# Two attentions with weights turned one step later, and the output product's first tiles begun between the last jobs

## What is computed

```
p = softmax(q @ k.T * scale + bias)          # 256 x 256 per head, causal
o = concat over heads of (p @ v)             # 256 x 1024
h = h + o @ w_out
```

## Time and profile before

| what | us |
|---|---|
| median of 3 runs (lowest, highest) | 1268.11 (1267.1, 1269.16) |
| the profiled execution's own time | 1271.67 |
| span of the profiled execution, first to last instruction | 1269.8 |
| PE busy | 1202.0 (95%) |
| DVE busy | 834.7 (66%) |
| ACT busy | 652.7 (51%) |
| POOL busy | 236.0 (19%) |
| first attention, first scores to last output ready | 90.2 to 147.6 |
| second attention | 424.6 to 458.3 |

### The profile page before, as it was taken

How to read it: one execution, slowest core, us unless ns; L and a number is a source line. 1 busy time by engine, 2 the same in 40 slices (tenths; PEclk the granted TensorE clock), 3 DMA queues, 4 the chain that set the end, 5 groups by cost and what they waited for, 6 DMA issues and landing times.

```text
span 1269.8 us, 19077 instructions
## 1 busy us (share of the span) xinstructions
PE 1202.0 (95%) x7698; PEld 1046.5 (82%) x7698; DVE 834.7 (66%) x1291; ACT 652.7 (51%) x1060; POOL 236.0 (19%) x300
## 2 busy tenths in 40 slices
PE   6898899999999889999999999999998789999996
PEld 5785588888888668888888889999996479888996
DVE  6955586666586567666557876457866856776643
ACT  6436566644333656664446555346545545655531
POOL 4103331110000232111112212000005510111101
PEclk9999999999999999999999999999999789999998
DMA  7790155564453424545554554652441023455461
GB/s 277 263 213 34 39 194 177 188 219 179 168 191 137 167 95 175 194 173 197 199 199 138 194 199 147 206 212 103 167 173 50 1 108 134 174 190 192 147 203 56
DMA packets 34088, 205.56 MB, mean 162 GB/s; under 512 B 3776, under 2 KB 6352, under 8 KB 13776
## 3 DMA queue, kind: packets, MB, share of 16 engines
q1 hardware_dynamic: 30704, 200.47, 44.3%
q10 hardware_dynamic: 3296, 3.87, 1.6%
HBM read 202.87 MB, written 1.46 MB: 161 GB/s over the span
## 4 chain that ended last, share of the span: by engine, by line
PE 79%; DVE 14%; ACT 3%; POOL 2%; issue 1%; DMA 1%; POOLq 0%; ACTq 0%; DVEq 0%
PE ps L662 36%; PE ps L667 23%; PE ps L665 5%; PE ps L666 5%; DVE wl L604 3%; PE ps L686 1%; PE ps L687 1%; PE ps L688 1%; DVE tf L2181 1%; POOL pb L965 1%; PE ps L909 1%; DVE y L1932 1%; DVE xb L740 1%; PE ps L1420 1%; ACT wh L575 1%
## 5 line engine op out<-in xcount | busy, mean ns | idle before, releaser
L604 DVE TENSOR_TENSOR wl<-raw,wh 128x2048 fp32r<-128x2048 f32 (+4 forms) x196 | 421.2, 2154 | 149.7 <-ACT wh L575 149.6
L662 PE MATMUL ps<-xb,wh 128*128 128x512 f32 x1424 | 502.8, 398 | 4.2 <-DVE wl L604 3.7
L667 PE MATMUL ps<-xb,wl 128*128 128x256 f32 x1696 | 477.1, 281 | 0.0
L575 ACT ACTIVATE wh<-raw 128x2048 fp32r<-128x2048 f32 (+4 forms) x196 | 348.5, 1781 | 153.3 <-PE ps L667 119.2
L662 PEld LDWEIGHTS ps<-xb,wh 128*128 128x128 f32 x1424 | 267.3, 188 | 70.5 <-issue 5.4
L667 PEld LDWEIGHTS ps<-xb,wl 128*128 128x128 f32 x1696 | 321.9, 190 | 0.0
L667 PE MATMUL ps<-ab,wl 128*128 128x256 f32 x1088 | 307.4, 283 | 0.0
L662 PE MATMUL ps<-ab,wh 128*128 128x512 f32 x640 | 226.8, 400 | 0.8 <-DVE ab L975 0.8
L667 PEld LDWEIGHTS ps<-ab,wl 128*128 128x128 f32 x1088 | 207.3, 191 | 0.0
L662 PEld LDWEIGHTS ps<-ab,wh 128*128 128x128 f32 x640 | 120.3, 188 | 31.7 <-DVE ab L975 1.4
L859 DVE TENSOR_TENSOR tf<-ps,tf 128x256 f32<-128x256 f32 x148 | 61.9, 421 | 119.6 <-ACT tf L854 119.6
(11 more groups left out here) (322 smaller groups left out, 1332.1 us busy)
## 6 DMA issues: line engine op xcount, KB each, us to landing
raw<-wstream SPq DMA_DIRECT2D x156, 1024.0 KB, 4.8
raw<-wstream SPq DMA_DIRECT2D x32, 704.0 KB, 4.0
raw<-wstream SPq DMA_DIRECT2D x8, 768.0 KB, 4.1
e_bt<-scratch ACTq DMA_DIRECT2D x16, 128.0 KB, 8.6
o_bt<-scratch SPq DMA_DIRECT2D x2, 1024.0 KB, 9.9
raw<-wstream SPq DMA_DIRECT2D x2, 560.0 KB, 7.2
raw<-wstream SPq DMA_DIRECT2D x4, 256.0 KB, 6.7
h<-xt ACTq DMA_DIRECT2D x4, 256.0 KB, 7.8
```

Source lines behind the costliest of these rows:

```text
L575: e.g.activation(WH[i % HLN][:, 0:w], RAW[i % RAWN][:, 0:w], ACT.Copy).then_inc(S["hi"], 1)
L604: e.g.tensor_tensor(WL[q][:, 0:w], RAW[i % RAWN][:, 0:w], f32(WH[q][:, 0:w]), ALU.subtract).then_inc(S["lo"], 1)
L662: e.g.matmul(PS[b][:, :].rearrange("p (a t) -> p a t", a=2), wh[:, sl], x2[:, :, cs], start=start, stop=k == p.nk - 1, skip_group_check=pair)
L667: ins = e.g.matmul(o, wl[:, sl], xh[:, cs], start=False, stop=k == p.nk - 1, skip_group_check=pair)
```

## The change

Turns, copies and outputs of both attentions happen one step later on every engine, the pv groups move from even to odd steps, and the compressed branch's extra work from step 11 to 12. `eo` and `oo` get banks 3 and 4 for their first two tiles, free with the maxima of job 21 (13); the new function `pe_begun` runs 12 of their blocks (k = 0 to 5 of tiles 0 and 1) in three portions of four at steps 22, 24 and 26 (14, 16 and 18), and the product itself starts at its 13th block. Since fixed banks don't advance the ring, all units behind eo take ring places two earlier, all behind oo four earlier.

```diff
-        Gemm("eo", "cols", 8, 8, 16, "h_eo", wide=True),
+        Gemm("eo", "cols", 8, 8, 16, "h_eo", fixed=(3, 4), wide=True),
...
-        Gemm("oo", "cols", 8, 8, 16, "h_oo", wide=True),
+        Gemm("oo", "cols", 8, 8, 16, "h_oo", fixed=(3, 4), wide=True),
...
-            "even": {3: (S["ex"], 24), 4: (S["ex"], 24), 0: (S["ol"], 7), 1: (S["ol"], 8), ...
-            "odd": {3: (S["ex"], 40), 4: (S["ex"], 40), ...
+            "even": {3: (S["mx"], 22), 4: (S["mx"], 22), 0: (S["ol"], 7), 1: (S["ol"], 8), ...
+            "odd": {3: (S["mx"], 38), 4: (S["mx"], 38), ...
-        def pe_cols(e, p, ks, xb, ready, after=None):
+        def pe_cols(e, p, ks, xb, ready, after=None, part=slice(None)):
...
-            for n, k, c, at, fresh, signals in p.blocks:
+            for n, k, c, at, fresh, signals in p.blocks[part]:
...
-            for i in range(A.n + 3):
+            for i in range(A.n + 4):
...
-                if 0 <= i - 2 < A.n and i % 2 == 0:
-                    act_turned(e, A, i - 2)
-                if 0 <= i - 3 < A.n and even_last(i - 3):
-                    d = even_pair(i - 3)
-                    act_out(e, d, PS[even_bank(d)][:, 0:256], i - 3 + 1, d)
+                if 0 <= i - 3 < A.n and i % 2:
+                    act_turned(e, A, i - 3)
+                if 0 <= i - 4 < A.n and even_last(i - 4):
+                    d = even_pair(i - 4)
+                    act_out(e, d, PS[even_bank(d)][:, 0:256], i - 4 + 1, d)
...
-            for i in range(A.n + 4):
+            for i in range(A.n + 5):
...
-                if i == 11:
+                if i == 12:
                     e.wait_ge(S["pcm"], 1)
...
-                if 0 <= i - 2 < A.n and i % 2:
-                    dve_turned(e, A, i - 2)
-                if 0 <= i - 4 < A.n and even_last(i - 4):
-                    d = even_pair(i - 4)
+                if 0 <= i - 3 < A.n and i % 2 == 0:
+                    dve_turned(e, A, i - 3)
+                if 0 <= i - 5 < A.n and even_last(i - 5):
+                    d = even_pair(i - 5)
                     dve_out(e, d, PS[even_bank(d)][:, 0:256], d)
...
-            for i in range(A.n + 3):
+            for i in range(A.n + 4):
...
-                if 0 <= i - 2 < A.n:
-                    if i - 2 < 2:
-                        e.wait(G["even"].free.get(A.turn_bank(i - 2)))
-                    pe_turn(e, A, i - 2)
-                if i % 2 == 0 and 0 <= i - 4 < A.n:
-                    pe_even_pv(e, i - 4)
-            pe_cols(e, G["eo"], range(8), AB, o_ready(0))
+                if 0 <= i - 3 < A.n:
+                    if i - 3 < 2:
+                        e.wait(G["even"].free.get(A.turn_bank(i - 3)))
+                    pe_turn(e, A, i - 3)
+                if i % 2 and 0 <= i - 5 < A.n:
+                    pe_even_pv(e, i - 5)
+                pe_begun(e, G["eo"], 0, {22: (0, 1), 24: (2, 3), 26: (4, 5)}.get(i, ()))
+            pe_cols(e, G["eo"], range(8), AB, o_ready(0), part=slice(12, None))
+
+        def pe_begun(e, p, base, tiles):
+
+
+            for k in tiles:
+                pe_cols(e, p, range(8), AB, o_ready(base), part=slice(2 * k, 2 * k + 2))
...
+                pe_begun(e, G["oo"], 8, {14: (0, 1), 16: (2, 3), 18: (4, 5)}.get(i, ()))
+            pe_cols(e, G["oo"], range(8), AB, o_ready(8), part=slice(12, None))
```

More of the change, by code:

```diff
@@ L392, in build @@
         end_of = count(products, S, {
-            "even": {3: (S["ex"], 24), 4: (S["ex"], 24), 0: (S["ol"], 7), 1: (S["ol"], 8), 2: (S["mx"], 24), 5: (S["pt"], 12), 6: (S["ptd"], 12)},
-            "odd": {3: (S["ex"], 40), 4: (S["ex"], 40), 0: (S["ol"], 8 + 7), 1: (S["ol"], 8 + 8), 2: (S["mx"], 40), 5: (S["pt"], 20), 6: (S["ptd"], 20)},
+            "even": {3: (S["mx"], 22), 4: (S["mx"], 22), 0: (S["ol"], 7), 1: (S["ol"], 8), 2: (S["mx"], 24), 5: (S["pt"], 12), 6: (S["ptd"], 12)},
+            "odd": {3: (S["mx"], 38), 4: (S["mx"], 38), 0: (S["ol"], 8 + 7), 1: (S["ol"], 8 + 8), 2: (S["mx"], 40), 5: (S["pt"], 20), 6: (S["ptd"], 20)},
             "mixer": {3: (S["sx"], 16), 4: (S["sx"], 16), 0: (S["oa"], 4), 1: (S["yd"], 8), 2: (S["ex"], 56), 5: (S["pt"], 28), 6: (S["nb_a"], 6)},
@@ L1631, in act_odd @@
                     act_exp_biased(e, A, i)
-                if 0 <= i - 2 < A.n and i % 2 == 0:
-                    act_turned(e, A, i - 2)
-                q = i - 3
+                if 0 <= i - 3 < A.n and i % 2:
+                    act_turned(e, A, i - 3)
+                q = i - 4
                 if 0 <= q < A.n and q % 2 == 1:
@@ L1663, in dve_odd @@
                     dve_reciprocal(e, A, i - 1)
-                if 0 <= i - 2 < A.n and i % 2:
-                    dve_turned(e, A, i - 2)
-                q = i - 4
+                if 0 <= i - 3 < A.n and i % 2 == 0:
+                    dve_turned(e, A, i - 3)
+                q = i - 5
                 if 0 <= q < A.n and q % 2 == 1:
@@ L1685, in pe_odd @@
             pe_odd_scores(e, 0)
-            for i in range(A.n + 3):
+            for i in range(A.n + 4):
                 if i % 2 and i + 1 < A.n:
                     pe_odd_scores(e, i + 1)
[L1689 to L1694, removed]
+                if 0 <= i - 3 < A.n:
+                    if i - 3 < 2:
+                        e.wait(G["odd"].free.get(A.turn_bank(i - 3)))
+                    pe_turn(e, A, i - 3)
+                q = i - 5
+                if i % 2 and 0 <= q < A.n:
                     d = q // 2
@@ L1710, in pe_odd @@
                                 ins.then_inc(S["pv"], 1)
-            pe_cols(e, G["oo"], range(8), AB, o_ready(8))
+                pe_begun(e, G["oo"], 8, {14: (0, 1), 16: (2, 3), 18: (4, 5)}.get(i, ()))
+            pe_cols(e, G["oo"], range(8), AB, o_ready(8), part=slice(12, None))
         def pe_odd_scores(e, h):
```

## The result

The changed kernel took **1248.1 us** (median of four runs, 1246.42 to 1249.7) beside 1268.18 us for the kernel before on the same chip (four runs, 1267.1 to 1269.16). The ratio is 0.9842 with a 95% interval of 0.9825 to 0.9859: 20.1 us less, between 17.9 and 22.2. The profiled execution of the new kernel took 1247.42 us (span 1245.6), that of the kernel before 1271.67.

The account below looks back on a forecast made before the run. PE, busy for 95% of the span, was taken as the bound, with only its idle time to win. Terms 9.2 + 1.7 + 2.2 + 3.4 = 16.5 us off the 1268.1 us median gave 1251.6 us, range 1247.0 to 1257.6.

Parts of the forecast that it names:

- The bound: Whole kernel: PE is busy for 95% of the span, so microseconds won in an attention should reach the end whole.
- Blocks, 9.2 us: Behind each attention's last output: 50 blocks left instead of 63, 4.6 us each, 9.2 us in all.
- Second attention, 1.7 us: Turns one step later there: middle gains 2.4 us, head loses 0.5, tail loses 0.2; bounds -1.5 and 3.1.
- First attention, 2.2 us: Turns one step later in the first attention's loop gain 2.2 us; bounds nothing and 3.6.
- Mo, 3.4 us: Mixer: mo's first unit gets bank 0, not 6, so mo starts earlier, gaining 3.4 us; bounds 1.9 and 4.3.
- with turns back to back it is about the 7.97 of now: Second attention's tail with the fill: 8.4 us at most, about 7.97 as before; 0.2 us taken as lost.
- rival 4: First attention: denser PE keeps the clock from falling at 121.0 to 124.6, 1.8 us more, 1249.8 us; chance 0.11.
- Rivals 1 and 5: Attention loops: turn waits return, loops gain nothing, 1255.5 us (0.14); or those waits become the bound, slower, 1277.5 us (0.03).
- Rival 2: Mixer: mo doesn't start earlier, or its gain is lost to clock or third chunk's supply, 1255.0 us; chance 0.09.
- Rival 3: Attention tails: fill not hidden, twelve blocks delay the last output by what they save, 1264.0 us; chance 0.04.
- The rule against the change: Attentions: POOL's weighings slowed beside DVE's weight pieces, up to 6.4 us, leaving the sum about 10 instead of 16.5.

Follow-up runs that it names:

- fill_only: Kernel before with the twelve early blocks and fixed banks in the old loops, turns not moved: 1260.73 us, ratio 0.9918.
- ring_mo: Kernel before with only the ring moved on by one place at mo: 1267.34 us, ratio 0.9984.
- fill_8: Changed kernel with eight early blocks instead of twelve: 1252.85 us, ratio 0.9858.
- lo_late: Changed kernel with DVE's low weight pieces of the second chunk moved to later steps in both attentions: 1248.85 us, ratio 0.9828.
- split_late: Changed kernel with the second chunk's low pieces on DVE and high pieces on ACT both moved to later steps: 1250.4 us, ratio 0.9841.
- mo_back: Changed kernel with the ring put back at mo, so mo and what follows have their old banks: 1253.67 us, ratio 0.9873.
- lag_only: Kernel before with only the turns one step later, no early blocks and no fixed banks: 1262.44 us, ratio 0.9936.
- after: The changed kernel itself, with the whole change against the kernel before: 1248.1 us, ratio 0.9842.
- banks_only: Kernel before with only eo's and oo's fixed banks, no early blocks and no turn moved: 1264.58 us, ratio 0.9951.

## Why the prediction was right, and what it missed

With the stretches of all runs, each term of the sum can be read by itself.

1. *The bound.* Time won in an attention does reach the end. The waits between the second attention and the mixer are the same three of L665, 2.6 us in all, beside 2.7 in the earlier trace rows.
2. *Blocks, 9.2 us.* Measured 4.6 (fill_only, "blocks 1", 277.03 to 272.43) and 4.7 ("blocks 2" at one pace, see the last section), 9.3. Right.
3. *Second attention, 1.7 us.* Measured 33.68 to 32.06, 1.6. By its parts: middle 4 x (4.04 - 3.47) = 2.3 (2.4 said); head from the first scores to the turn of job 4, 9.6 to 10.3 us, so 0.7 lost (0.5 said); tail from the turn of job 12 to the ready output, 447.28 - 439.35 = 7.93 beside 7.97, nothing lost (0.2 said). Right.
4. *First attention, 2.2 us.* Without the fall of the clock (point 6) the old loops take 44.71 us (ring_mo) and the new ones 42.86: 1.85. Right.
5. *Mo, 3.4 us.* "End" mixes the bank with PE's pace: behind mo, PE ran at the slower of its two paces (last section) in the kernel before, fill_8, lo_late and split_late, and mostly at the faster one in the other eight, which is worth 1.8 us. Less these 1.8, "end" is 247.3 in the kernel before, 247.3 in mo_back and 246.4 in lag_only with the old bank, and 243.1 to 243.5 us in the nine profiles with the new one, 243.2 on average: 3.2 to 4.1 us, and 3.9 by the times of mo_back against after. Right. A part of it is the clock. In the kernel before and in mo_back it had come back and fell again during the wait of 3.49 us, so that mo began at the lower level; in no profile with the new bank does it fall there. The kernel before, around 1022.3 us (us, PE, PEld, DVE, ACT, POOL busy, granted clock, DMA):

```profile
1019.00:1022.20 3.20, 0.70 (x2) 0.30 (x2) 3.06 (x7) 1.22 (x3) 0.80 (x1) 1.00 0.00 0
1022.40:1029.00 6.60, 4.42 (x20) 4.42 (x21) 4.98 (x13) 3.68 (x7) 0.00 (x0) 0.50 0.00 0
```

The prediction let the clock come back 4.6 us behind mo's start whenever it starts. In the profiled changed kernel it took 4.2, but in five of the nine profiles with the new bank the clock was full when mo began. In each of these five PE then stood 0.3 us for an input and 0.5 us for weights, and "end" came out the same to 0.4 us.

The terms as measured sum to 9.3 + 1.6 + 1.85 + 3.2 to 4.1 = 16.0 to 16.9 us, and I had said 16.5.

**Where I was wrong inside a sum that came out.** I had the later turn and the fill as separate prices: the turn worth some 4 us (2.4 - 0.5, and 2.2), the fill costing 0.2. The comparison of lag_only with before and after prices them anew. The turn is worth 2.5 (33.68 to 31.17) and 4.0 (44.71 to 40.73), 6.5 us. The fill costs 0.9 and 2.1, 3.0 us. The failed reading was "with turns back to back it is about the 7.97 of now": I set the filled tail against the tail of the kernel before, and forgot that the later turn shortens an unfilled tail too, to 448.39 - 441.37 = 7.02 us. The expectation for lag_only rested on that split and was too small by half. The fill is also kinder to the new loops than to the old: 4.3 us in the old (fill_only, 2.0 and 2.3), 3.0 in the new. That the two parts help each other by 1.3 us stood nowhere in my sum. The turn is worth 2.4 us more than my price and the fill costs 2.8 us more; that these two errors nearly cancel was luck as far as the parts go.

6. *What the sum left out: rival 4.* I gave 0.11 to the clock staying up in the first attention, and it did. PE's windows of the earlier trace rows have a granted clock of 0.53 from 121.0 to 124.6. Of the four profiles with the old loops two show that fall (before and banks_only) and two don't, and "first" is 46.10 and 45.83 us there against 44.71 in ring_mo. None of the eight profiles with the later turn does. The fall is worth 1.1 to 1.4 us (1.8 said). What PE does before it does not tell whether it comes. The windows of the kernel before, then of fill_only, each the same distance behind ev1's end (columns as above):

```profile
117.00:121.00 4.00, 2.77 (x22) 1.53 (x22) 3.81 (x17) 2.72 (x10) 1.91 (x5) 1.00 0.01 2
```

```profile
117.50:121.50 4.00, 2.78 (x22) 1.53 (x22) 3.81 (x17) 2.73 (x10) 1.91 (x5) 1.00 0.01 2
121.00:124.60 3.60, 3.28 (x30) 1.87 (x28) 2.64 (x15) 3.28 (x11) 2.31 (x4) 1.00 0.40 118
```

PE was busy for 2.77 us of 4 in the one and 2.78 in the other, and only in the first did the clock fall. The same stretch has 2.77 in banks_only, where it fell, and 2.78 in ring_mo, where it didn't. With the later turn PE does 16.35 us of work in the 19.6 us behind ev1's end instead of 14.65, so the rival's denser PE is there; yet the least busy four microseconds in that stretch are 2.63 or 2.64 in all twelve profiles. None of eight profiles against two of four fits the rival, but that the density is the reason stays argued, not shown.

**The balance.** 16.5 + 1.4 = 17.9 us against 20.1 measured, at the lower end of its interval. The same sums for the parts give 7.9 for lag_only (8.1 measured) and, where its profile shows no fall of the clock, 10.1 for fill_only (10.4 measured). The profiled pair closes: of its 24.2 us, 16.6 are the terms (3.8 for mo), 1.4 the fall in the first attention, 4.0 the pace ("blocks 1" 0.4, "blocks 2" 1.8, "end" 1.8) and 2.1 the two stretches that the change does not touch. "Scores to ev1" took 8.8 to 11.7 us and "mixer" 56.5 to 58.2 over the twelve profiles, by the stretches at the lower clock, in old and new kernels alike.

The 2 us that the medians have beyond the terms are not priced by any run, but the record shows where they may lie. The mean granted clock of every run is known: 0.978 to 0.987 in 39 runs of the kernel before, mean 0.983, and 0.986 to 0.988 in the eight of the changed kernel, mean 0.987; on one chip 0.982 (mean of 9 runs) beside 0.987 to 0.988 (4). The traces have two levels, 1.00 and 0.50, so an estimate of the time at the lower one is twice what the mean lacks to 1, times the span: 44 us in an execution of the kernel before and 31 in one of the changed kernel. With mo's old banks (mo_back) it is 0.983 to 0.984 in six runs. So the change does shift the odds of the clock, by more than the one fall of rival 4, and mo's banks have a large part in it; what each of these microseconds costs was not measured.

*Rivals 1 and 5* fell. The maximum L926 waits for a turn once, during ev1, and never in the middle. *Rival 2* fell by mo's rows. *Rival 3* was half true in mechanism: the fill costs 3.0 us, not the 8.5 of its price. *The rule against the change* did not bite. In the second attention POOL's weighings (L965) next to a piece of weights take longer, as in the earlier trace rows. The meetings did become more, against my count of no change: in both attentions together 20 of the 80 operations of L965 fall beside a piece instead of 10. Yet all of them take 39.8 us instead of 39.2, POOL's busy time over the whole span is 236.3 us against 236.0, and the 6.4 us did not occur. The sharing that the Trainium skill (GPSIMD Engine Reference, Specifications) describes is there in these rows: in the second attention of the changed kernel an operation beside a piece takes up to 0.95 us, the others at most 0.48. It cost little, and DVE's queue, not POOL, was what PE's turns depended on.

## What to carry to other kernels

When one engine is nearly full, price a fill against the idle time that is left once the other parts of the change are in, not against the kernel before; two lines, the sum of PE's waits in front of the last output and the length of the filled work, gave the cost within 0.2 us in the second attention and 0.5 in the first. A fixed order of banks is part of the schedule: look at every wait of a product's first matmul for which *bank* it waits, because moving the ring by one place removed 3.5 us of waiting far from the edited loop. And after a ring of waits has been widened, ask at once which engine is the new floor: taking DVE's pieces of weights out of the middle shortened the two attentions by another 2.1 us.

## What I had not expected of the hardware

**PE has two paces at the same granted clock.** "Blocks 2" differed by up to 3.8 us between kernels with the same work in it (498.14 after, 501.91 in fill_only). The cause is seen in the windows from 500 to 550 us, where both kernels run the same kind of blocks (one 512-column and one 256-column matmul) with PE full and the clock at 1.00. First the changed kernel, then lag_only:

```profile
500.00:550.00 50.00, 50.00 (x291) 43.70 (x290) 32.11 (x37) 32.65 (x46) 9.37 (x9) 1.00 0.53 192
```

```profile
500.00:550.00 50.00, 50.00 (x285) 43.38 (x284) 32.09 (x36) 32.40 (x45) 9.36 (x9) 1.00 0.53 188
```

291 matmuls against 285 in 50 us. Blocks start 0.347 us apart in the one and 0.353 to 0.354 in the other, 1.9% more, and a pace holds for some hundred microseconds. The other engines' work and the DMA share are alike. Over the wide products of "blocks 2", the kernel before ran about 104 us at the faster pace, the changed one some 200, lag_only, ring_mo and fill_only none, the rest 104. If each such stretch is set to the slower pace (times 0.019), "blocks 2" becomes 506.5, 506.6, 506.6 and 505.8 us for before, lag_only, ring_mo and banks_only, and 501.8 to 501.9 for all seven profiles with twelve early blocks, fill_8 lying between with 503.0. That is the 4.7 us used above, and it takes 1.8 us out of the profiled pair. "End" shows the same two paces: 243.1 to 243.5 us in six profiles with mo's new bank and 244.9 to 245.0 in three. What sets the pace no run here shows: the same kernel, run again, had 104 us of it in "blocks 2" instead of 200.

**The clock fell behind a PE that was working.** In the kernel before, PE was busy for 69% of the four microseconds before 121.0 us (2.77), none of its waits between 112 and 121 us was longer than 1.23, and the granted clock then fell to the lower level (1.2 GHz). The same work in front of the same place was followed by a fall in two profiles and by none in two.
